# Forget sums of the third layer: from selector products on TensorE to masks filled by transfers and GpSimd

## What is computed

```python
def fox_mixer(h, w_in, b_f, w_o):
    ...
    log_f = jax.nn.log_sigmoid(f_logit + b_f)
    lc = jnp.cumsum(log_f, axis=1).transpose(0, 2, 1)
    ...
        s = jnp.einsum('bhqd,bhkd->bhqk', q[:, :, t0:t1], k[:, :, :t1]) * (hd ** -0.5)
        s = s + lc[:, :, t0:t1, None] - lc[:, :, None, :t1]
        mask = jnp.arange(t1)[None, :] <= (t0 + jnp.arange(blk))[:, None]
        p = jax.nn.softmax(jnp.where(mask[None, None], s, -jnp.inf), axis=-1)
```

## Time and profile before

| what | value |
|---|---|
| median of 3 runs | 1579.52 us |
| the profiled execution, its own time | 1579.89 us |
| its span | 1578.1 us |
| granted TensorE clock, mean | 0.993 of full speed |
| TensorE matmul, busy | 1524.4 us (97%) |
| VectorE, busy | 1189.8 us (75%) |
| ScalarE, busy | 797.3 us (51%) |
| GpSimd, busy | 109.4 us (7%) |
| mixer of the third layer, where the pairs stand | 682.7 to 763 us of the span |

### The profile page before, as it was taken

How to read it: one execution, slowest core, us unless ns; L and a number is a source line. 1 busy time by engine, 2 the same in 40 slices (tenths; PEclk the granted TensorE clock), 3 DMA queues, 4 the chain that set the end, 5 groups by cost and what they waited for, 6 DMA issues and landing times.

```text
span 1578.1 us, 24612 instructions
## 1 busy us (share of the span) xinstructions
PE 1524.4 (97%) x9348; PEld 1320.8 (84%) x9348; DVE 1189.8 (75%) x1776; ACT 797.3 (51%) x1093; POOL 109.4 (7%) x111
## 2 busy tenths in 40 slices
PE   2989999999999999999999999999999999999999
PEld 1868888889988888899888888788888888889998
DVE  6887877789589777765697777969777787676666
ACT  2454444356464443565543435565344667665544
POOL 0150000000000000011000000220000063200000
PEclk8999999999999999999999999999999999999999
DMA  9946877956258888573478885446888655345550
GB/s 388 367 140 263 322 292 294 396 190 238 81 214 325 329 304 330 213 256 134 161 315 338 304 321 212 147 160 263 339 326 306 231 182 179 121 152 198 184 186 27
DMA packets 54910, 383.80 MB, mean 243 GB/s; under 512 B 6420, under 2 KB 6932, under 8 KB 9264
## 3 DMA queue, kind: packets, MB, share of 16 engines
q1 hardware_dynamic: 50976, 363.75, 61.3%
q0 software_dynamic: 3856, 18.97, 3.4%
HBM read 381.62 MB, written 4.22 MB: 245 GB/s over the span
## 4 chain that ended last, share of the span: by engine, by line
PE 87%; DVE 6%; DMA 3%; ACT 1%; issue 1%; POOL 1%; SPq 0%; ACTq 0%; DVEq 0%
PE PS L2498 30%; PE PS L2068 25%; PE PS L2554 17%; PE PS L2089 3%; PE PS L2219 2%; DMA CST<-cst_in 1%; PE PS L2294 1%; PE PS L2269 1%; DMA adar<-ada 1%; PE PS L2532 1%; DVE wlo L1474 1%; DVE adar L1499 1%; PE PS L2246 1%; DMA raw<-ada 1%; PE PS L2199 1%
## 5 line engine op out<-in xcount | busy, mean ns | idle before, releaser
L1474 DVE TENSOR_TENSOR wlo<-raw,whi 128x2048 fp32r<-128x2048 f32 x225 | 516.6, 2297 | 135.1 <-ACT whi L987 134.8
L987 ACT ACTIVATE whi<-raw 128x2048 fp32r<-128x2048 f32 x230 | 438.8, 1911 | 185.4 <-PE PS L2554 116.9
L2068 PE MATMUL PS<-hhi,whi 128*128 128x256 f32 x1040 | 300.1, 289 | 1.5 <-DVE wlo L1474 1.5
L2068 PE MATMUL PS<-hlo,whi 128*128 128x256 f32 x1040 | 294.8, 283 | 0.0
L2068 PE MATMUL PS<-hhi,wlo 128*128 128x256 f32 x1040 | 294.7, 283 | 0.0
L1499 DVE CUSTOM_DVE_ANT_0 adar<-adar,CB 128x1024 f32<-128x1024 f32 x232 | 276.2, 1231 | 10.0 <-DMA adar<-ada 10.0
L2498 PE MATMUL PS<-whi,hhi 128*128 128x512 f32 x704 | 278.9, 396 | 1.9 <-DVE hlo L1572 1.0
L2498 PE MATMUL PS<-whi,hlo 128*128 128x512 f32 x704 | 274.8, 390 | 0.0
L2498 PE MATMUL PS<-wlo,hhi 128*128 128x512 f32 x704 | 274.4, 390 | 0.0
L2068 PEld LDWEIGHTS PS<-hhi,whi 128*128 128x128 f32 x1040 | 199.9, 192 | 8.1 <-issue 7.2
L2068 PEld LDWEIGHTS PS<-hlo,whi 128*128 128x128 f32 x1040 | 199.9, 192 | 1.7 <-issue 1.2
(11 more groups left out here) (269 smaller groups left out, 2110.3 us busy)
## 6 DMA issues: line engine op xcount, KB each, us to landing
raw<-weights SPq DMA_DIRECT2D x234, 1024.0 KB, 6.8
adar<-ada SPq DMA_DIRECT2D x104, 1024.0 KB, 5.1
adar<-ada POOLq DMA_DIRECT2D x12, 1024.0 KB, 5.2
raw<-ada SPq DMA_DIRECT2D x4, 1024.0 KB, 15.3
bias_rows<-bias_of_distance POOLq DMA_DIRECT2D x1, 3072.0 KB, 16.6
adar<-bias_rows POOLq DMA_DIRECT2D x8, 256.0 KB, 3.4
CST<-cst_in SPq DMA_DIRECT2D x1, 1128.0 KB, 22.7
CB<-c_in SPq DMA_DIRECT2D x2, 512.0 KB, 4.1
```

Source lines behind the costliest of these rows:

```text
L987: act.activation(whi[:, u % CV, :], raw[:, u % RAW, :], ACT.Copy).then_inc(hi_done, 1)
L1474: v.tensor_tensor(wlo[:, u % CV, :], raw[:, u % RAW, :], whi[:, u % CV, :].bitcast(F32), ALU.subtract).then_inc(lo_done, 1)
L2068: m = pe.matmul(o, w(a), h(b), start=first and k_ == 0, stop=last and k_ == 2, skip_group_check=True)
```

## The change

`scores(p)` has no selector products and no wait for `lc_lo`. `SEL`, `LCK`, the constant they need (16 columns of `CST`) and the four instructions that fill them (three of ScalarE, one of VectorE) are gone. The 16 rows of `LC` are stored to device memory by a transfer of GpSimd's queue. For each pair two transfers of the same queue bring the rows of its two heads back, each repeated over all 128 partitions, into one of two buffers in `SCR` (`forget_mask`). GpSimd adds the causal mask to the two blocks of 128 columns that need it (`forget_add`), and `mask_max(p)` reads this buffer in place of the constants, after a wait on `lc_mask`.

```diff
+        def forget_mask(p):
+
+            return two(flat_scr[:, 768 * (p % 2):768 * (p % 2) + 768])
...
-                if kind in ("swa", "fox"):
+                def forget_load(p):
+
+                    if p >= 2:
+                        pool.wait_ge(s_masked, pos0[l] + p - 1)
+                    for a, b in segments(kind):
+                        src = bass.AP(tensor=rows.tensor, offset=2 * p * S, ap=[[0, P], [S, 2], [1, b - a]])
+                        pool.dma_start(forget_mask(p)[:, :, a:b], src).then_inc(lc_in[p % 2], 16)
+
+                def forget_add(p):
+
+                    pool.wait_ge(lc_in[p % 2], 32 * (p // 2 + 1))
+                    ends = forget_mask(p).rearrange("p h (k s) -> p h k s", s=P)
+                    below = cst("masks", P).unsqueeze(1).to_broadcast([P, 2, P])
+                    pool.tensor_tensor(ends[:, :, 0, :], ends[:, :, 0, :], below, ALU.add)
+                    pool.tensor_tensor(ends[:, :, 2, :], ends[:, :, 2, :], below, ALU.add).then_inc(lc_mask, 1)
+
+                if kind == "fox":
+                    pool.wait_ge(bias_spread, 16)
+                    pool.wait_ge(lc_done, 2)
+                    pool.dma_start(bass.AP(tensor=rows.tensor, offset=0, ap=[[S, 16], [1, S]]), LC[:, 2, :]).then_inc(lc_out, 16)
+                    pool.wait_ge(lc_out, 16)
+                    forget_load(0)
+                    forget_load(1)
+                    forget_add(0)
+                    forget_add(1)
+                    for p in range(PAIRS):
+                        if p + 2 < PAIRS:
+                            forget_load(p + 2)
+                        normalise(p)
+                        if p + 2 < PAIRS:
+                            forget_add(p + 2)
+                if kind == "swa":
                     for p in range(PAIRS):
                         normalise(p)
...
-                    act.activation(LCK, LCK.bitcast(F32), ACT.Copy, scale=0.0).then_inc(lc_hi, 1)
-                    act.activation(SEL[:], cst("heads", 16), ACT.Copy).then_inc(lc_hi, 1)
...
-                    act.wait_ge(lc_done, 2)
-                    act.wait_ge(lc_hi, 2)
-                    act.activation(LCK[0:16, :], LC[:, 2, :], ACT.Copy).then_inc(lc_hi, 1)
...
-                        mask = cst("masks", n, 0 if kind == "fox" else 2 * P)
+                        if kind == "fox":
+                            v.wait_ge(lc_mask, p + 1)
...
+                                mask = forget_mask(p)[:, h, :] if kind == "fox" else cst("masks", n, 2 * P)
...
-                    v.wait_ge(lc_hi, 3)
-                    v.tensor_tensor(LCK[32:48, :], LC[:, 2, :], LCK[0:16, :].bitcast(F32), ALU.subtract).then_inc(lc_lo, 1)
...
-                            m = pe.matmul(part(h, q), QT[r, p, P * q:P * q + P], KT[r, kt, 0:n], start=q == 0, stop=kind != "fox", skip_group_check=True)
-                    if kind == "fox":
-                        for h in range(2):
-                            sel = SEL[:, 2 * p + h:2 * p + h + 1]
-                            for q in range(2):
-                                m = pe.matmul(part(h, q), sel.to_broadcast([P, P]), LCK[:, 0:P * (q + 1)], start=False, stop=True, skip_group_check=True)
+                            m = pe.matmul(part(h, q), QT[r, p, P * q:P * q + P], KT[r, kt, 0:n], start=q == 0, stop=True, skip_group_check=True)
...
-                    pe.wait_ge(lc_lo, 1)
```

More of the change, by code:

```diff
@@ L74 @@
 CST_AT, CST_N = columns([("ones", P), ("ident", P), ("cos", S), ("sin", S), ("perm", P), ("halves", P),
-                         ("masks", 5 * P), ("chunk", 64), ("lncount", 2 * S), ("reset", S), ("heads", 16)])
+                         ("masks", 5 * P), ("chunk", 64), ("lncount", 2 * S), ("reset", S)])
 PAR_AT, PAR_N = columns([("ada_b", 48 * 5), ("gain", 8 * 11), ("conv", 16 * STEPS), ("qkn", 4),
@@ L175, in program @@
         RD = sb("RD", [P, 2, 4])
-        SEL = sb("SEL", [P, 16], F32R)
         eps_both = sb("eps_both", [P, 4 + C])
@@ L196, in program @@
         LC = flat_scr[0:16, 0:3 * S].rearrange("p (a b) -> p a b", a=3)
-        LCK = alo[:, 1, S:2 * S]
+        def forget_mask(p):
+            return two(flat_scr[:, 768 * (p % 2):768 * (p % 2) + 768])
         ALOW = adar[0:16, 1, 1024:1024 + S]
@@ L245, in program @@
         small_pe, lc_done, lc_act = sem("narrow_projection"), sem("log_forget_vec"), sem("log_forget_act")
-        lc_hi, lc_lo = sem("log_forget_hi"), sem("log_forget_lo")
+        lc_out, lc_mask = sem("log_forget_stored"), sem("forget_masks_added")
+        lc_in = [sem(f"log_forget_repeated{i}") for i in range(2)]
         s_ready, s_masked, st_max, att_exp, att_den = (
@@ L2648, in constants @@
     put("reset", np.broadcast_to((t % 64 != 0) * 1.0, (P, S)))
-    put("heads", ((p[:, None] % 32 == np.arange(16)[None, :]) & (p[:, None] < 64)) * 1.0)
     onehot = np.zeros((32, 512), np.float32)
```

## The result

| | median us | lowest to highest | runs |
|---|---|---|---|
| before | 1579.47 | 1577.82 to 1582.26 | 20 |
| changed | 1583.34 | 1579.65 to 1586.36 | 20 |

The ratio changed to before is 1.0021, with a 95% interval from 1.0014 to 1.0027: the change makes the kernel slower, by 3.9 us between the medians. The forecast was 1576.5 us, and 1583.34 lies above its range. The profiled execution of the changed kernel took 1583.94 us, 4.05 more than that of before.

A forecast was written before the change was run, and what follows sets the result against it. TensorE was taken to bound the third layer's mixer without a gap. Seven pairs' gains and 0.2 us of wait, -7 x 0.46 + 0.2 = -3.0 us, took the median 1579.52 to 1576.5 us, range 1575.7 to 1578.8.

The forecast's parts named there:

- The gain of 0.46 us a pair: On TensorE behind each pair's scores, removing selector products shortens 1.53 us to 1.08, giving back 0.45 to 0.46 us.
- The tail's claim on the eighth pair: TensorE's wait before values(5) grows from 1.07 to 1.5 us, leaving 3.2 us; rival without this loss, chance 0.12.
- The selectors were not hidden: Against the rival that TensorE keeps its distance from scores to the next unit without selectors: about 1579.5 us, chance 0.05.
- filling `LCK` and `SEL` was free: Removing the three ScalarE and one VectorE instructions that filled these buffers was taken at zero, since nobody on the path waits.
- GpSimd and VectorE hold each other: At pair 0's additions, each waits up to 1.15 us and holds the next VectorE instruction up to 0.6 us.
- The 10 us: By the skill's rule, additions of all pairs could hold VectorE for 16 x 0.6 = 10 us in all.
- Step "Store of 16 rows": On GpSimd's queue after the sums at 675.4, the store takes 3.0 to 3.5 us, so loads begin at about 678.7.
- Step "Loads of pair 0": On GpSimd's queue, pair 0's loads land 4.5 us after the second issue at 679.4, so at 683.9.
- the first mask is very late: Rival: loads land after 15.2 us, scores(1) waits 7.8 us, 1584.1 us; slower once mask_max(0) ends after 692.7; chance 0.06.
- The two additions: On GpSimd for pair 0, behind the loads landing at 683.9, both are done at about 686.8.
- Step "Later pairs": From pair 1 on, masks are in time; normalise(1) may run 1 us late with 8 us of room: zero cost.

The follow-up runs named there:

- run 1: This name does not occur in <kept>, and the text calls no run or kernel by it.
- nothing added: The changed kernel without the wait for masks and without GpSimd's store, loads and additions, so only the selector products are gone: 1576.3 us, ratio 0.9978.
- held weights: The changed kernel with SyncE holding unit 9's weights in the third layer, and all behind them, until the loads of pairs 0 and 1 landed: 1579.95 us.
- the new order: On top of held weights, GpSimd's additions for pair p+1 stand behind normalise(p), in place of those for pair p+2: 1576.34 us, ratio 0.9973.
- the second profile: The changed kernel measured once more, with no edit, beside the kernel before on the same chip: 1581.78 us, ratio 1.0012.
- filler: The changed kernel with 40 products of 256 columns into a free bank ahead of scores(1), where TensorE would wait: 1582.38 us, ratio 1.0014.
- SyncE's queue: The changed kernel with the store and the loads of pairs 0 and 1 on SyncE's queue, and additions in the new order: 1579.02 us, ratio 0.9995.
- the second experiment: The changed kernel with mask_max reading the constant mask and not waiting for the additions; store, loads and additions stay: 1581.64 us, ratio 1.0018.
- two pairs by selectors: The kernel before for pairs 0 and 1, the changed kernel for pairs 2 to 7: 1576.33 us, ratio 0.9979.

## Why the prediction was wrong

**What held.** The gain of 0.46 us a pair: 1.08 us from scores to the second product, and -3.26 us with nothing added. The tail's claim on the eighth pair: 1.07 became 1.55. The selectors were not hidden, and filling `LCK` and `SEL` was free. GpSimd and VectorE hold each other, as the prediction said: the additions took 0.71 to 2.17 us, and VectorE's lo beside GpSimd's normalise 2.93 in place of 2.29:

```profile
699.62 2.93 DVE L1504 TENSOR_TENSOR wlo<-raw,whi 128x2048 fp32r<-128x2048 f32 x1
```

The rule of the Trainium skill that the prediction named (SBUF — State Buffer, Who interferes with whom), that a VectorE instruction with two inputs in SBUF and a GpSimd instruction that reads SBUF shut each other out, agrees with these times. The 10 us that the prediction worked out for VectorE did not come: in the layer with held weights and the new order nothing of it reached TensorE, -3.25 against -3.26 with no additions at all.

**Step "Store of 16 rows", taken at 3.0 to 3.5 us: wrong.** It landed after 5.9 (4.6 in the second profile), and from the sums (676.01) to the first load (682.74) it was 6.7 us. The row I leaned on, comes from a quieter place: the transfer engines were 0.69 busy while that store was under way and 0.90 while this one was. The earlier trace rows with a share of 0.97 made me add half a microsecond at most. With the weights held, at 0.11, the same store landed after 1.7, and with the new order, at 0.10, after 2.8.

**Step "Loads of pair 0", taken at 4.5 us: wrong.** The second load of pair 0 landed after 8.6 us, pair 1's last after 10.5. I had put them nearer to the fifth layer's 2.3 to 5.5 than to the 8.3 to 15.2 of the earlier trace rows, by their size. But what counted was what was sent just in front of them and among them: the 1 MB transfers from 674.60 to 684.70, which SyncE's timeline of the kernel before already had at 673.96 to 684.05. With these held, the same loads took 3.9 to 4.7, just what I had taken. The Trainium skill's price (DMA: Bandwidth & Descriptors, Anatomy of one DMA) would be, as an estimate, 2.0 us for the store and 2.9 for a pair; the trace disagrees by 3.9 us for the store. With the weights held the store comes near it (1.7 and 2.8 us), the loads, at 3.9 to 4.7, stay above.

Both together put mask_max(0) at 693.67 in place of 687.3 to 688. TensorE would have been at scores(1) at 690.2 (695.02 - 4.84), against 689.5 in the forecast; scores(0) itself began 0.64 us later. The rival "the first mask is very late" names this mechanism and its turning point, a mask that ends 3.2 us behind TensorE; it got 0.06, since it was tied to the worst landing of the earlier trace rows alone and not to two moderate delays in series, 3.4 us at the store (6.7 against 3.3) and 4.1 at the load (8.6 against 4.5), that add up. The two additions took back about 1.5 us: done 1.4 us behind the load, where 2.9 had been taken.

**Step "Later pairs", "Zero for all of it": wrong.** It looked at normalise(1) and gave it 8 us of room. Not looked at was normalise(0), which on GpSimd stands behind the additions of pair 1 and so behind the latest of the four loads. TensorE waited 3.2 us for it when the mask was not waited for, and 0.9 and 2.2 us for normalise(1) and normalise(2) when the first loads were fast. For a late mask it is hidden under the first wait.

**In the same step, blocking in the wrong place.** The prediction let GpSimd's additions and VectorE hold each other, and gave normalise(1) 1 us. Not looked at was what lo does to a normalise that comes late. Its multiply took 3.10 or 3.11 us in place of 1.03 where it ran beside lo, 2.07 us more; line 924 of the kernel before had a longest of 3.09 us too, in another layer. TensorE's waits for such a normalise were 1.6 (filler), 1.4 (SyncE's queue) and 0.9 us (held weights), all shorter than that, while the 2.2 us of the held weights at pair 2 were hardly longer. The 3.2 us of the second experiment have nothing of it, since normalise(0) took 1.04 there. With the new order and the weights held no normalise met lo. How much of the waits is blocking and how much the place in the list no run separates, since one brings the other.

**Missing from the sum: the clock.** At the end of TensorE's wait of 4.84 us (3.7 in the second profile) the granted clock was at half for 3.4 us. The prediction priced a wait at its length. Here it cost 1.7 us more, though the filler showed that these 1.7 and the wait for normalise(0) cover each other: without either of them one would still pay the other.

**Open.** Where the clock drops elsewhere in the program, and why in some executions only, isn't explained; the medians of the changed kernel, 1583.34 and 1581.78, lie 1.6 us apart, and how much of that is the clock and how much the landing of store and loads isn't shown. Not tried were the new order of additions without the held weights and a third buffer for the masks.

## What to carry to other kernels

Price a small transfer by what its neighbours' queues have under way at that moment, and read that from the issue list of the engine that issues them; a median from a quieter layer is off by a factor of two, and a chain of store and load pays it twice. Where an in-order engine both waits for transfers and does work that the bottleneck waits for, look at every instruction queued behind each new wait, and put what is ready first. Then look beside which instruction of the other engine it comes to stand. If only the first of several steps can't be fed in time, keep the old way for those: two pairs by selectors kept 2.35 of 3.26 us without holding back a single weight.

## What was unexpected of the hardware

- A store of 16 KB landed after 1.7, 2.8, 4.6, 5.1 and 5.9 us in five profiles (weights held, the same with the new order, the changed kernel again, SyncE's queue, the changed kernel). In the first two no 1 MB transfer had been sent in the 5 us before it, in the other three one 1.5 to 2 us before it. Between 1.7 and 2.8 nothing here explains the difference: the transfer engines were 0.11 and 0.10 busy.
- The granted clock fell to half at the end of waits of TensorE of 4.84, 3.7 and 3.2 us, each time for 3.4 us, and not behind waits of 1.6 (filler) and 2.2 us (held weights).
- GpSimd's multiply of 128x512 took 3.11 us in place of 1.03 beside VectorE's lo, which itself took 2.93 in place of 2.29.
